# Prompt attention on one core: the value products of two key tiles side by side, in the second and fourth quarter of a step

## The reference

```python
lc = jnp.einsum('ntghd,ncgd->ntghc', qg, kc) + bc
pc = masked_softmax(lc, (dc >= 0)[:, None, None, :])
oc = jnp.einsum('ntghc,ncgd->ntghd', pc, vc)
...
ps = masked_softmax(ls.reshape(n, tq, g, hpg, kk * sb),
                    (ds >= 0).reshape(n, tq, g, 1, kk * sb))
osel = jnp.einsum('ntghjs,ntgjsd->ntghd', ps.reshape(n, tq, g, hpg, kk, sb), vsel)
...
pw = masked_softmax(lw, mw[:, None, None, :])
ow = jnp.einsum('ntghk,nkgd->ntghd', pw, vw)
o = gt[..., 0:1] * oc + gt[..., 1:2] * osel + gt[..., 2:3] * ow
```

## Time and profile before

| | us |
|---|---|
| median of three runs | 2365.25 |
| lowest and highest | 2365.06, 2369.87 |
| the profiled execution | 2369.16 |
| its span, first to last instruction | 2367.5 |
| PE matmul busy | 2265.3 (96%) |
| POOL, DVE, ACT busy | 1099.7, 1073.0, 580.9 |

### The profile page before, as it was taken

One profiled execution on the slowest core, in us unless ns is written; L12 is line 12 of the kernel. 1 busy time (PEld: TensorE's weight loads), 2 busy tenths in 40 slices (PEclk: granted clock), 3 DMA queues, 4 the chain that ended last, 5 costly groups with the idle time before them and its releaser, 6 DMA issues. The chain is left out here.

```text
span 2367.5 us, 37799 instructions
## 1 busy us (share of the span) xinstructions
PE 2265.3 (96%) x14824; PEld 1694.0 (72%) x14824; DVE 1073.0 (45%) x2077; ACT 580.9 (25%) x1340; POOL 1099.7 (46%) x980
## 2 busy tenths in 40 slices
PE   9898999899999999999998999999999999999997
PEld 7675555476777777677776777686776777777776
DVE  5343665326330340367886556453643154313322
ACT  2003675402000000145554323332420010000011
POOL 3211554157654574465655233322426365644653
PEclk9999999999999999999999999999999999999998
DMA  9724001821112121311221030200203112112211
GB/s 326 217 92 160 1 1 36 307 73 72 71 62 99 72 72 71 138 55 60 70 73 56 6 108 7 99 11 25 89 23 129 72 71 74 69 72 95 83 72 40
DMA packets 55883, 197.16 MB, mean 83 GB/s; under 512 B 15458, under 2 KB 29538, under 8 KB 39714
## 3 DMA queue, kind: packets, MB, share of 16 engines
q1 hardware_dynamic: 49186, 177.52, 21.3%
q0 software_dynamic: 3088, 14.03, 1.8%
q10 hardware_dynamic: 3440, 3.25, 0.4%
HBM read 170.86 MB, written 32.17 MB: 86 GB/s over the span
## 5 line engine op out<-in xcount | busy, mean ns | idle before, releaser
L1969 PE MATMUL ps<-xn,ring 128*128 128x288 f32 x768 | 198.9, 407 | 4.3 <-DVE xn L2072 3.2
L1969 PE MATMUL ps<-hid,ring 128*128 128x288 f32 x768 | 192.8, 406 | 0.0
L1969 PEld LDWEIGHTS ps<-xn,ring 128*128 128x128 f32 x768 | 145.5, 190 | 47.0 <-DVE xn L2072 5.9
L1969 PEld LDWEIGHTS ps<-hid,ring 128*128 128x128 f32 x768 | 145.8, 190 | 40.4 <-ACT p L2006 0.8
L2052 POOL TENSOR_TENSOR prod<-prod,rstd 128x1152 f32<-128x1152 f32 x32 | 83.9, 2621 | 179.7 <-DVE prod L2136 163.4
L2006 ACT ACTIVATE p<-ps 128x288 f32<-128x288 f32 x48 | 19.7, 410 | 597.4 <-PE ps L1969 597.4
L3381 PE MATMUL ps<-xn,ring 128*128 128x288 f32 x512 | 137.1, 415 | 3.6 <-PE ps L3450 3.6
L1969 PE MATMUL ps<-x_sum,wsum 128*128 128x288 f32 x512 | 132.0, 411 | 3.0 <-DVE x_sum L2076 1.9
L1022 POOL TENSOR_SCALAR ring<-ring,fac 128x128 f32<-128x128 f32 (+2 forms) x96 | 92.3, 976 | 88.2 <-DVE fac L1263 88.2
L1969 PE MATMUL ps<-hid_sum,wsum 128*128 128x288 f32 x512 | 128.4, 407 | 0.2
L2026 POOL TENSOR_TENSOR wsum<-ring 128x512 f32<-128x512 f32 x64 | 81.8, 1279 | 100.0 <-DMA ring<-in_w_mlp 92.1
(11 more groups left out here) (531 smaller groups left out, 4952.0 us busy)
## 6 DMA issues: line engine op xcount, KB each, us to landing
ring<-in_w_mlp SPq DMA_DIRECT2D x64, 1024.0 KB, 4.8
ring<-in_w_gdn_in SPq DMA_DIRECT2D x16, 1024.0 KB, 4.8
ring<-in_w_nsa_in SPq DMA_DIRECT2D x9, 1024.0 KB, 17.0
ring<-in_w_gdn_z SPq DMA_DIRECT2D x8, 1024.0 KB, 5.7
x<-in_seq_state SPq DMA_DIRECT2D x4, 2048.0 KB, 9.0
out_seq_state<-x SPq DMA_DIRECT2D x4, 2048.0 KB, 11.0
ring<-in_w_gdn_out SPq DMA_DIRECT2D x8, 1024.0 KB, 5.5
out_win_old<-in_win_rows POOLq DMA_DIRECT2D x1, 8064.0 KB, 47.4
```

What stands on the lines that cost most here:

```text
L1969: mm = nc.tensor.matmul(S.ps[:, base + BANK[p], 0:HT], stationary(p, blk.units[pair // 4], pair % 4), moving(blk.kind, p, pair), start=pai ...
```

## The change

In PE's program alone, the value products of quarter s are left out for even s, and for odd s those of key tiles s - 1 and s stand one behind the other, after the scores of quarter s and before its transpose chunk.

```diff
--- before.py
+++ after.py
@@ -1113,7 +1113,8 @@
                         qk(step, s)
                     if step < 2:
                         keep_busy(S, 1, OB + 1)
-                    if 0 <= step - 3:
+                    if 0 <= step - 3 and s % 2:
+                        times_v(step - 3, s - 1)
                         times_v(step - 3, s)
                     if s < 3 and 0 <= step - 2 < NJ:
                         turn(step - 2, s)
```

## The result

The changed kernel takes **2375.24 us** (median of 14 runs, 2369.92 to 2379.16), the kernel before 2365.4 in the runs beside them (median of 14, 2360.26 to 2369.87). The ratio is 1.0041, with a 95% interval of 1.0031 to 1.0051: slower by 9.8 us, between 7.3 and 12.1. The profiled execution took 2376.01, its span 2374.4. The forecast was 2371.7, its sum +6.4.

The account below looks back on a forecast made before the run. PE, 96% busy, was taken to be bound in a near-balanced ring with DVE and ACT. Step 3's 0.86, six pairs of 0.75 and 1.1 for steps 16 and 17 gave +6.4 on 2365.25: 2371.7, range 2366.0 to 2377.0.

Parts of the forecast that it names:

- the ring through PE, DVE and ACT: Prompt attention: a pair of steps is a ring of waits near balance; each next pair starts 0.75 us later.
- its allowance for the clock: Whole run: two fewer to three more slow stretches of the granted clock, -3.1 to +4.7 us.
- The bounds by the links alone: Waits between engines, without the clock: 3.9 to 7.4 us longer, so 2369.1 to 2372.7.
- Joints of 0.15: Adjacent value groups on PE: 0.15 us saved at each joint, 29 joints, 4.4 us less work.
- The result by joints alone: Rival: ACT and DVE give way, so PE's saved work comes through in full, 2360.9; chance 0.08.
- Even step: Third scores start 0.15 earlier, PE idles 0.8 before the third transposes, fourth scores stay, the next step begins 0.43 later.
- The exps come 0.1 earlier: Odd step's second scores, waiting for exps of the step before: start 0.1 earlier, between 0 and 0.15.
- the upper bound of the link, 0.86: Start of the next pair: 0.86 us later if the exps come no earlier, in place of 0.75.
- The link of 3.79: Odd step: compressed transposes follow the third scores' start by 3.79 us; PE itself needs 3.51, so 0.28 more idling.
- Steps 16 and 17: Steps without scores: waits of about 0.8, 0.40 and 0.40 before transposes; 12.8 against 11.74, +1.1 us.
- a rival of 0.10: The clock drops more often: three more slow stretches on top of the sum, 6.4 + 4.7, so 2376.4; chance 0.10.
- The wash: Rival: compressed transposes' link gives, exps come earlier, a slow stretch is missed; +0 to +4, some 2367.5; chance 0.28.

Follow-up runs that it names:

- E1: Kernel before, with only the value products of key tiles 0 and 1 together, in quarter 1; tiles 2 and 3 as before: 2373.68 us, ratio 1.0047.
- E3: Kernel before, with the changed order of value products in odd steps only: 2374.35 us, ratio 1.0049.
- E4: Kernel before, with the changed order of value products in even steps only: 2363.63 us, ratio 0.9999.
- E8: Kernel before, with value products of tiles 0 and 1 together in quarter 0, of 2 and 3 in quarter 2: 2363.07 us, ratio 0.9998.
- E5: Changed kernel, with DVE's second half of the compressed softmax a quarter earlier and ACT's compressed exp moved ahead for it: 2363.94 us, ratio 1.0004 to the kernel before.
- E7: Kernel before, with E5's move on DVE and ACT and E8's order of value products on PE: 2360.47 us, ratio 0.9985.
- E6: Kernel before, with E5's move on DVE and ACT alone, PE's order unchanged: 2359.41 us, ratio 0.9984.
- E9: Kernel before, with the first half of odd steps' second scores also waiting for the exp that frees the second half: 2364.67 us, ratio 1.0004.
- E2: Kernel before, with only the value products of tiles 2 and 3 together, in quarter 3; tiles 0 and 1 as before: 2366.26 us, ratio 1.0010.

## Why the prediction was right or wrong

- **Direction and mechanism: right.** Slower, by the ring through PE, DVE and ACT, with the loss between second and third scores of the odd step. E1, E3 and E4 place it there, E8 has the same joints elsewhere and loses nothing, and E5 makes up for the loss by freeing the second scores earlier.
- **The number: inside the range by its allowance for the clock.** The bounds by the links alone ended at 2372.7, 2.5 below the result. That the range reached 2377.0 was owed to more slow stretches of the clock, for which I gave in part the wrong reason (below). To that extent it was luck.
- **Joints of 0.15: right.** The joined groups are 1.66 and 0.80 from start to start. In a pair PE is busy 0.42 less, of 0.60 forecast; busy times are modelled and overlap, so the starts are the better measure. The result by joints alone (2360.9) didn't come, as forecast, since PE's work wasn't what set the length. The Trainium skill (TensorEngine Tiling, Key Properties) says that changing the tiling mode drains TensorE. The 0.15 agrees with that, but no run shows that the drain is what a joint saves. Where PE is nearly the bound, E7 gets 0.10 of a pair from the joints.
- **Even step: wrong in its parts, right in what lasts.** The third transposes idle 0.62, not 0.8, since the second transposes themselves come 0.13 slower behind ACT's copy at 288.93 (0.94 from start to start, not 0.81). So the third scores come at 6.05, as before, not 0.15 earlier.
- **"The exps come 0.1 earlier": this step failed.** They come no earlier (12.33 against 12.32): with the third scores unmoved, DVE has nothing sooner. I had set the upper bound of the link, 0.86, for just this case. That makes 0.87 for 0.75, six times over: 0.7 us.
- **The link of 3.79: right**, 3.80 in the change and in E5. PE's own way was 3.58 with 0.22 of idling, not 3.51 with 0.28.
- **Steps 16 and 17: 1.25 for 1.1.** From start to start the three waits took 0.92, 0.41 and 0.40, for 0.8, 0.4 and 0.4; the idle times by the records are 0.84, 0.34 and 0.34:

```profile
400.76 1.11 PE L1072 MATMUL ps<-cst,ring 128*128 128x128 f32 x8 [0.84 <-ACT cprobt L1168]
...
404.67 0.90 PE L1072 MATMUL ps<-cst,ring 128*128 128x128 f32 x6 [0.34 <-ACT probt L1155]
...
410.19 0.90 PE L1072 MATMUL ps<-cst,ring 128*128 128x128 f32 x6 [0.34 <-ACT probt L1155]
```

- **The clock: the term left at zero.** The sum of 6.4 should have been 7.3 by the links, and the clock most likely gave the rest, some 2.5. I let it widen the range and gave it a rival of 0.10, and that rival's number (2376.4) is nearer to the result than the forecast's. But its first reason, transposes right behind the compressed scores, isn't borne out: E4 and E5 have that order and no more slow stretches. Its second, the 1.6 of idling in a pair, is nearer: the added stretches stand behind long waits. The Trainium skill (TensorE: Matmul & The Clock Gate, Part 4) says that the full clock doesn't engage for transposes. Steps 16 and 17, nearly half transposes, run at 1.00.
- **The wash: it didn't come.** The link to the compressed transposes gave nothing, nor did the exps.

## What to carry to other kernels

An engine that is 96% busy may still not set the length: lay its groups from start to start against a fixed mark, and look for the group that takes longer than its size, since such a group is being held. Work put behind a held group and ahead of what the other engines wait for costs its full length (0.86 here), and the same work elsewhere costs nothing (E8). The better edit is to release the held group, here by moving 1.9 us of DVE's work a quarter forward (E6, 3.4 us below the kernel before). And an edit made on top of such a release is measured against the release alone (E5 against E6, not E5 against the kernel before).

## What the runs showed of the hardware

- Two score products of 64 rows run side by side if they are released together: both 256-column halves take 0.64 (E6, E9). Released one after the other they take 1.30, 1.29 in the change, and 0.90 in E2, where the first comes later. In the kernel before, in E2 and in E9 the group ends at the same point, 13.61 to 13.63 after the pair's start, so delaying the first half until the second is free costs nothing (E9).
- A neighbouring value group is worth 0.15 us at each joint, in the stage at full clock, whether it stands in the second, fourth, first or third quarter (1.65 to 1.66 for 512 and 384 columns, 0.80 to 0.81 for 256 and 128).
- Where PE waits for it, PE starts 0.63 us after ACT begins a pair of copies of 384 columns, in the kernel before, in the change and in E5; behind copies of 512 columns it was 0.75 in E8.
- Medians of one kernel differ by up to 2.6 us between sets of runs (2362.84 to 2365.4 for the kernel before), and its single runs lie from 2357.97 to 2372.4. A difference of 1 us, such as E2's, is seen in the windows and not in the times.
